# Two whole expert loads split into one of 96 partitions and four of 8 partitions

## What is computed

```python
def expert_block(args):
    xb, e = args
    return (jax.nn.silu(xb @ w_gate[e]) * (xb @ w_up[e])) @ w_down[e]
```

## Time and profile before

| what | value |
|---|---|
| median of three runs | 1111.54 us |
| the profiled execution | 1112.12 us |
| its span, first to last instruction | 1110.3 us |
| PE busy | 1012.5 us (91%) |
| POOL, DVE, ACT busy | 494.3, 507.4, 380.5 us |
| DMA moved | 342.09 MB, mean 308 GB/s |
| PE's part of the chain that ended last | 69% |
| DMA's part of it | 21% |

### The profile page before, as it was taken

The page is one execution under the profiler, slowest core; times in us unless marked ns, Lnnn a source line. Parts: engine busy times, 40 slices in busy tenths (PEclk is TensorE's granted clock), DMA queues, the critical chain, the costliest instruction groups (busy, mean ns, idle before and its releaser), DMA issues.

```text
span 1110.3 us, 18626 instructions
## 1 busy us (share of the span) xinstructions
PE 1012.5 (91%) x7938; PEld 765.3 (69%) x7938; DVE 507.4 (46%) x905; ACT 380.5 (34%) x540; POOL 494.3 (45%) x209
## 2 busy tenths in 40 slices
PE   7999999999999999999999999899998777878676
PEld 6989988788799999887999895344443333434232
DVE  1998987566357678123445643322331212212113
ACT  7345545644563444356585341000000000000002
POOL 6987799879588888967664410000000000000000
PEclk9999999999999999999999999999999999999998
DMA  9754455457369999728334879999999999999993
GB/s 383 267 189 157 151 194 206 166 202 308 125 252 361 349 353 352 307 76 335 142 141 149 329 320 398 415 425 426 425 426 428 424 429 423 429 425 428 424 423 161
DMA packets 38535, 342.09 MB, mean 308 GB/s; under 512 B 4273, under 2 KB 4657, under 8 KB 6322
## 3 DMA queue, kind: packets, MB, share of 16 engines
q1 hardware_dynamic: 37152, 337.56, 76.0%
q10 hardware_dynamic: 1298, 3.32, 0.8%
HBM read 339.81 MB, written 1.05 MB: 307 GB/s over the span
## 4 chain that ended last, share of the span: by engine, by line
PE 69%; DMA 21%; DVE 5%; ACT 2%; SPq 1%; issue 1%; POOL 0%; DVEq 0%; ACTq 0%
DMA ring<-in_gu 20%; PE ps L527 16%; PE ps L528 16%; PE ps L529 16%; PE ps L1147 6%; PE ps L1194 5%; PE ps L1183 2%; SPq L2494 1%; PE ps L1127 1%; PE ps L520 1%; PE ps L709 1%; DVE rd L2184 1%; DVE ar L2372 1%; PE ps L909 1%; ACT ar L1711 0%
## 5 line engine op out<-in xcount | busy, mean ns | idle before, releaser
L2438 POOL TENSOR_TENSOR spl<-raw,sph 128x1024 fp32r<-128x1024 f32 x204 | 493.9, 2453 | 150.5 <-ACT sph L1251 150.4
L1251 ACT ACTIVATE sph<-raw 128x1024 fp32r<-128x1024 f32 x204 | 208.0, 1056 | 117.3 <-PE ps L529 88.5
L527 PE MATMUL ps<-xbh,sph 128*128 128x256 f32 x480 | 136.6, 285 | 3.7 <-DVE xbl L1783 2.0
L528 PE MATMUL ps<-xbl,sph 128*128 128x256 f32 x480 | 135.8, 283 | 0.0
L529 PE MATMUL ps<-xbh,spl 128*128 128x256 f32 x480 | 135.8, 283 | 0.0
L2372 DVE TENSOR_TENSOR ar<-ar,ps 64x256 f32<-64x256 f32 x32 | 13.5, 422 | 261.0 <-ACT ar L1711 261.0
L1711 ACT ACTIVATE ar<-ps 64x256 f32<-64x256 f32 x32 | 12.1, 377 | 331.5 <-PE ps L1147 331.5
L1194 PE MATMUL ps<-ar,ar 128*128 128x512 f32 x256 | 120.1, 612 | 0.0
L527 PEld LDWEIGHTS ps<-xbh,sph 128*128 128x128 f32 x480 | 92.1, 192 | 4.8 <-DVE ar L2122 2.2
L527 PE MATMUL ps<-xah,sph 128*128 128x256 f32 x320 | 91.9, 287 | 1.1 <-DVE xal L1773 0.8
L528 PEld LDWEIGHTS ps<-xbl,sph 128*128 128x128 f32 x480 | 92.1, 192 | 0.0
(11 more groups left out here) (310 smaller groups left out, 1630.3 us busy)
## 6 DMA issues: line engine op xcount, KB each, us to landing
raw<-in_stream SPq DMA_DIRECT2D x127, 1024.0 KB, 5.8
ring<-in_gu SPq DMA_DIRECT2D x46, 2048.0 KB, 44.6
ring<-in_dn SPq DMA_DIRECT2D x22, 2048.0 KB, 45.0
ring<-in_gu SPq DMA_DIRECT2D x24, 1024.0 KB, 10.8
ring<-in_dn SPq DMA_DIRECT2D x14, 1024.0 KB, 9.2
ar<-in_gu SPq DMA_DIRECT2D x7, 1024.0 KB, 25.2
slotx<-in_gu SPq DMA_DIRECT2D x5, 1024.0 KB, 37.6
ar<-in_dn SPq DMA_DIRECT2D x3, 1024.0 KB, 48.1
```

The costliest lines, as they stand in the source:

```text
L527: e.matmul(o, sh, mh, start=start, stop=False)
L528: e.matmul(o, sh, ml, start=False, stop=False)
L1251: e.activation(u.half(SPH[u.n % NSP], h), u.half(RAW[u.slot], h), ACTF.Copy).then_inc(w.up(hi_ok), 1)
L2438: e.tensor_tensor(u.half(SPLO[u.n % NSP], h), u.half(RAW[u.slot], h), u.half(SPH[u.n % NSP], h), ALU.subtract).then_inc(w.up(lo_ok), 1)
```

## The change

For two pieces, s = 120 and s = 142, the one load of 128 partitions becomes five: partitions 0 to 95 in one, then 96 to 103, 104 to 111, 112 to 119 and 120 to 127. All five add 16 to the same semaphore, so the count rises by 80 for these two. Both go to the buffer `ring3`. Piece 120 is the third of expert 20 (so pieces 120 and 121 are the second half of its gate and up weights), piece 142 the first of expert 24. Bytes, destinations, waits and all other loads stay as they are.

```diff
+        def by_eights(s):
+
+            return s in (120, 142)
+
...
             if paired(s) and i % 2:
                 slot_landed[entry] = slot_sem[i - 1], per_slot[i - 1]
             else:
-                per_slot[i] += 16
+                per_slot[i] += 80 if by_eights(s) else 16
                 slot_landed[entry] = slot_sem[i], per_slot[i]
...
                     if i % 2 == 0:
                         consumed(s)
                         consumed(s + 1)
-                        e.dma_start(WHOLE[i // 2], expert_whole(I, s)).then_inc(slot_sem[i], 16)
+                        cuts = [0, 96, 104, 112, 120, 128] if by_eights(s) else [0, 128]
+                        for a, b in zip(cuts, cuts[1:]):
+                            e.dma_start(WHOLE[i // 2][a:b, :], expert_whole(I, s)[a:b, :]).then_inc(slot_sem[i], 16)
```

## The result

The changed kernel takes **1135.18 us** (median of four runs, 1133.97 to 1136.74) against 1110.78 us before (four runs, 1108.01 to 1111.76). The ratio is 1.0226, 95% interval 1.0207 to 1.0244: 24.4 us slower, 12.2 us for each of the two loads. The forecast was 1125 us, with a range from 1110 to 1135, so the result lies just above its upper end.

What follows compares the result with a forecast made beforehand. The expert stage was taken as bound by its loads. Crowded small transfers summed to 17.3 us for two loads, discounted to 13.6 us and added to the 1111.54 us median: 1125 us, range 1110 to 1135.

Steps and rivals of the forecast that it cites:

- What bounds the kernel: TensorE bounds up to 700 us; the expert stage ends bound by its loads, whose last landing moves the end one for one.
- Issues at nothing: Eight more issues hold SP 3.8 us in all, 1.9 us a load, hidden by a lead of 47 us.
- Rows moved, 2.47 us: In both cut loads eight engines carry 10 rows and the others 6, instead of 8: 2.47 us for both.
- A small transfer at 2.47 us: Each eight-partition transfer, 131 KB, was priced at 2.47 us, between 0.62 us and 4.95 us.
- two-inlet case: Middle price of a small transfer: eight neighbouring partitions fill through two inlets of 26.5 GB/s, so 2.47 us.
- cheap end: Lowest price of a small transfer: each row goes as fast as in a whole load, 0.62 us.
- The 96-partition transfer at 6 x 0.62 = 3.7 us: In each cut load the large transfer gives every engine 6 rows at a whole load's 0.62 us a row.
- Three quarters of the way: Engines not quite in step crowd less: 2.47 + 0.75 x (17.3 - 2.47) = 13.6 us for both loads, not 17.3.
- Half share for 15 us or more: Sign of crowding: at the end of the stream the DMA share stays near 0.5 for 15 us or more.
- it pays: Rival: cheap small transfers ride on the engines that finish first, last landing 0.9 us earlier, 1110.6 us; chance 0.18.
- late engines are hit: Rival: cheap small transfers give a late engine 2.5 us more at the stream's end, 1114.0 us; chance 0.15.
- nothing happens: Rival: small transfers go to changing engines or rows are cut over all sixteen, 1111.5 us; chance 0.12.

Runs made afterwards that it cites:

- experiment 6: Kernel before with the two loads cut into even and odd partitions, 1111.36 us; in another run into two column halves, 1110.63 us; both against 1111.15.
- experiment 4: Kernel before plus fourteen groups of loads behind its last store, each waiting for the one ahead: 96 partitions 8.68 us, 128 partitions 7.73 us.
- experiment 2: Changed kernel with the four small transfers joined, so each load goes as 96 and 32 partitions: 1128.29 us, ratio 1.0149 to the kernel before.
- experiment 7: Kernel before, two loads cut into partitions 0-63 and 64-127: 1127.60 us; another run, small transfers before load groups: 96 + 32 adds 4.4, 6.4, 7.2 us.

## Why the prediction was right in kind and wrong in size

**What bounds the kernel.** Right. The first and longest stage did not change, and the loss lies where the loads are the bound: 23.2 us by the two dips, 22.5 us at the end of the same execution. A loss there went to the end one for one, as forecast.

**Issues at nothing.** Nothing speaks against it. SP was held longer than said, 6.8 us more at the first cut and not 1.9, but the DMA share stayed at 1.01 through both dips and the lead at some 50 us. One more issue a load was free (experiment 6); four more were not tried by themselves.

**Rows moved, 2.47 us.** The premise held: eight signals for eight partitions. Its share in the loss was not separated in the kernel.

**A small transfer at 2.47 us.** The number held in a stream, where four cost 9.5 us or 2.4 each, and neighbours were dearer than spread ones, as the two-inlet case supposed; the rows of 3.68 and 2.96 us show that the destination matters. But two inlets don't explain all of it. Spread over four apart, the same transfers cost 1.2 us each in the stream and not the 0.62 of the cheap end. By themselves, four neighbours took 9.18 us and one 3.71, so a further one costs 1.8 us. That the middle case met 2.4 is in part luck.

**The 96-partition transfer at 6 x 0.62 = 3.7 us.** This is the step that failed. In the sum "6 x 0.62 + 4 x 2.47" its rows go at the speed of a whole load's rows. They don't: 7.2 us in a stream, and 8.68 alone against 7.73 for the whole load. I counted rows for each engine and used the argument of the shared inlet for the small transfers only. It holds for 96 neighbours as well: by the layout of ports cited in experiment 4 they fill one half of the ports fully and the other by half. That alone would make 8 x 0.62 = 4.95 us in place of 3.7. The expectation of experiment 2 reckoned so, and it was far too low: at most 5 us for both loads, where 16.8 were measured. That neighbours are what costs is shown by halves against even and odd partitions. Why 96 of them cost 7.2 us and not 4.95 is open.

**Three quarters of the way.** The discount from 17.3 to 13.6 us had no counterpart: the kernel lost 24.4 us, more than the full sum. "Engines that arrive apart do not crowd each other" is not tested by experiment 7, though. There the small transfers in front give the same row more to each of eight engines, and the discount spoke of these eight being spread among themselves. What it shows is that what stands in front can make a cut dearer, for the five from 11.4 to 13.0 us. Whether the state of the kernel's engines makes the difference between 5.0 and 8.4 us for 96 + 32 isn't shown.

In the prediction's own sum the two steps are worth 2 x (7.2 - 3.7) = 7.0 us and 17.3 - 13.6 = 3.7 us. Together with its 13.6 this gives 24.3 us, beside the 24.4 measured. The agreement is closer than the terms deserve, since each price from a stream is good to some 0.5 us a load. The groups with all five say the same less sharply: 2 x 11.4 = 22.8 us, or 2 x 13.0 = 26.0 behind small transfers.

**The signs.** The dips (915 to 930 us forecast, 908 to 932 found; the second from 972) and the waits of 5 to 9 us for the two cut loads (5.35 and 7.83) came as named. The waits of 7.39 and 8.67 us for the loads ahead of them were not foreseen. "Half share for 15 us or more, because the half without small transfers is done long before" did not. The rate fell below half in the dips themselves, so more than one half was slowed. The 96-partition transfer, which had been priced as harmless, has rows on all sixteen engines.

**The rivals.** That it pays, that late engines are hit, that nothing happens: the first two needed a small transfer at the cheap end, under 0.73 us, and it cost 2.4. The third foretold no change; the packets show that a row is not cut over all engines, and whether the four small transfers take the same eight they do not tell.

## What to carry to other kernels

Whole loads of all 128 partitions ran at 424 GB/s in this kernel. A load cut by partitions kept that only where each piece was spread over the whole: even and odd partitions were free, and so was a cut by columns. Halves of neighbours cost 8 us a load here, and a piece of 96 partitions took longer than all 128. So before a load is cut, price every piece by which partitions it fills, the large piece too, and not by its bytes.

## What the runs showed that was not expected

- 96 partitions of 16 KB took 8.68 us and 128 took 7.73, alone and one behind the other.
- The slowing reaches beyond the cut load: a dip of 24 us at 227 GB/s for a load of 4.95 us, with the DMA share at 1.01 all the while. The whole load ahead of the cut one is late as well. A full share says that the engines are held, not that they move much.
- Small transfers in front of the whole loads raise the price of a badly cut load, from 4.4 to 7.2 us. Why is open.
- Spreading the four small transfers saves 4.7 us a load in a stream by itself and 1.5 us in the kernel.
